# A decoder layer with product-key experts: the norm's share of the expert turns, the projection's opening block, attention's rooms and the queries' end changed

## The reference, cut to what matters

```python
n1 = rms_norm(x, norm1_w) * (1 + sc1) + sh1
h = n1 @ w_in                       # 1024 x 8704: recurrence q|f|i|g, attention q|k|v, two gates
oa = hgrn_chunked(q, 1 - f, i, log f, S0) ; ya = (rms_norm(oa) * silu(g)) @ w_branch_a
ob = three dilated window attentions, merged by their softmax sums ; yb = ob @ w_branch_b
x = x + g1 * ((sigmoid(ga) * ya + sigmoid(gb) * yb) @ w_out)
n2 = rms_norm(x, norm2_w) * (1 + sc2) + sh2
# experts, for every token: 8 heads, each takes the best 16 of 128 x 128 product keys
q = rms_norm((n2 @ peer_wq) per head) ; s1, s2 = q @ k1.T, q @ k2.T ; eidx, g = top16(s1 + s2)
x = x + g2 * sum over heads and picks of g * gelu(n2 . u[eidx]) * v[eidx]
```

## Time and profile before

| what | number |
|---|---|
| median of three runs | 4373.25 us |
| the profiled execution's own time | 4375.05 us |
| its span | 4373.3 us |
| busy in the span | PE 3063.8, DVE 2572.8, ACT 1940.2, POOL 1446.6 us |
| moved by all DMA queues | 1454.06 MB, 332 GB/s over the span |
| moved by the gathers' queue | 1107.36 MB, 62.6% of 16 engines' time |
| mean granted TensorE clock | 0.824 |

### The profile page before, as it was taken

One profiled execution on the slowest core, in us unless ns is written; L12 is line 12 of the kernel. 1 busy time (PEld: TensorE's weight loads), 2 busy tenths in 40 slices (PEclk: granted clock), 3 DMA queues, 4 the chain that ended last, 5 costly groups with the idle time before them and its releaser, 6 DMA issues. The chain is left out here.

```text
span 4373.3 us, 46875 instructions
## 1 busy us (share of the span) xinstructions
PE 3063.8 (70%) x14244; PEld 1663.8 (38%) x14244; DVE 2572.8 (59%) x6558; ACT 1940.2 (44%) x6708; POOL 1446.6 (33%) x1174
## 2 busy tenths in 40 slices
PE   7999877784898998566654686885555556555556
PEld 5677754641553446344432464551111111111111
DVE  2362335377566755584654545467667766766774
ACT  2123431045457844574542225445455555545554
POOL 4453102352332333232211113335244344334432
PEclk9998889886999999666876797887777776777879
DMA  7434245388999999787999988999999999999997
GB/s 281 185 142 138 83 142 179 112 354 335 364 406 377 422 421 401 287 334 274 382 360 361 344 308 312 381 368 386 403 420 420 415 409 420 420 404 419 417 407 308
DMA packets 313887, 1454.06 MB, mean 332 GB/s; under 512 B 41609, under 2 KB 102977, under 8 KB 165282
## 3 DMA queue, kind: packets, MB, share of 16 engines
q0 software_dynamic: 152064, 1107.36, 62.6%
q1 hardware_dynamic: 147118, 336.43, 21.7%
q10 hardware_dynamic: 14452, 7.26, 0.6%
HBM read 1383.55 MB, written 74.57 MB: 333 GB/s over the span
## 5 line engine op out<-in xcount | busy, mean ns | idle before, releaser
L3249 POOL DMA_INDIRECT uv_ring<-in_peer_uv,pick_idx x736 | 794.9, 1080 | 1853.4 <-PE expert_acc L3421 1355.2
L3421 PE MATMUL expert_acc<-uv_ring,diag 128*32 128x512 f32 (+1 forms) x2888 | 714.4, 781 | 424.8 <-ACT diag L3386 373.3
L3344 DVE SCALAR_TENSOR_TENSOR uv_ring<-uv_ring,n_pairs 128x1024 f32<-128x1024 f32 x534 | 651.2, 1232 | 410.0 <-DMA uv_ring<-in_peer_uv,pick_idx 339.1
L3373 ACT ACTIVATE gelu_cube<-dots_now 128x2 f32<-128x2 f32 x528 | 105.7, 200 | 1017.8 <-DVE uv_ring L3344 589.9
L3421 PEld LDWEIGHTS expert_acc<-uv_ring,diag 128*32 128x32 f32 (+1 forms) x2888 | 154.8, 149 | 886.0 <-ACT diag L3386 544.6
L3381 ACT ACTIVATE pick_weight<-gelu_tanh,pick_share 128x1 f32<-128x1 f32 x1056 | 350.9, 379 | 23.1 <-ACT pick_share L3378 4.1
L3421 PE MATMUL expert_acc<-uv_tail,diag 128*64 128x512 f32 x608 | 215.4, 847 | 171.6 <-ACT diag L3386 150.3
L3344 DVE SCALAR_TENSOR_TENSOR uv_ring<-uv_ring,n_more 128x1024 f32<-128x1024 f32 x202 | 243.7, 1222 | 144.8 <-DMA uv_ring<-in_peer_uv,pick_idx 111.6
L997 PE MATMUL h_acc_q<-in_w_all_q,n_all_q 128*128 128x512 f32 x640 | 285.1, 601 | 4.0 <-DVE h_stage_q L971 3.7
L3376 ACT ACTIVATE gelu_tanh<-gelu_cube,dots_now 128x1 f32<-128x1 f32 x1056 | 253.3, 287 | 16.3
L3378 ACT ACTIVATE pick_share<-dots_now,pick_prob 128x1 f32<-128x1 f32 x1056 | 245.4, 280 | 0.0
(11 more groups left out here) (491 smaller groups left out, 5876.7 us busy)
## 6 DMA issues: line engine op xcount, KB each, us to landing
in_w_p<-in_w_in SPq DMA_DIRECT2D x34, 1024.0 KB, 7.4
in_w_all_q<-in_w_in SPq DMA_DIRECT2D x17, 2048.0 KB
ada_w<-in_w_ada SPq DMA_DIRECT2D x10, 2048.0 KB, 8.2
past_keys_q<-in_past_keys SPq DMA_DIRECT2D x16, 1024.0 KB
uv_ring<-in_peer_uv,pick_idx POOLq DMA_INDIRECT x736
shared_room_q<-in_past_values SPq DMA_DIRECT2D x10, 1024.0 KB
score_pair<-scores SPq DMA_DIRECT2D x66, 128.0 KB
wq_raw_p<-in_peer_wq SPq DMA_DIRECT2D x16, 512.0 KB, 5.8
```

Of the source, the lines that this page charges most:

```text
L3249: pool.indirect_dma_start(self.rows_of(part, s), None, self.x["peer_uv"][0], bass.IndirectOffsetOnAxis(ap=self.idx[:, q % 2, 2 * half + s, ...
L3344: ins = dve.scalar_tensor_tensor(out=row, in0=row, scalar=1.0, in1=n2[:, s if tile < LAST_TILE else 0, :], op0=ALU.mult, op1=ALU.mult, acc ...
L3373: link(act.activation(self.cube[:], dots, ACT.Square))
L3421: ins = pe.matmul(self.acc[s * w:(s + 1) * w, c, :], self.diag[:, of % DIAGS, t, 0:w], rows, start=first, stop=last)
```

## The change: what it does

1. **Norm.** In span q's first norm the nominal cost per tile is 5.0 in place of 9.0 on all engines (`share`); other norms keep 9.0.
2. **Opening block.** The projection's block 0 (2 MB) is loaded by SP into the shared room during that norm, behind the first two tiles' rows and the shifts (`SharedRoom.first`). The projection loads blocks 1 and 2 at its start, and block n + 1 from block 2 on. PE takes block 0 out of the room. POOL waits before block 1 until block 0's units are done, and the slot in the room opens at part 41 instead of 33. DVE waits for the rotary tables only before its first QK unit.
3. **Rooms.** The places of raw queries, raw values and the second state output in the shared room are exchanged; the second state output moves into the chunk tables. In attention, SP issues keys(1), the query rows and both past blocks 0 and 1 before it waits for the state stores; the wait now stands before values(1).
4. **Queries' end.** `LAST_TURNS` = 2 further turns are put at the end of the query phase: on PE one after the third of the last head's rows and one behind the head, on the other engines both behind it. `FRONT_PARTS` becomes 259, the tail's slots open two parts later, and `FRONT_US` becomes 2116.87 x 235 / 233, a rate of 0.11007.
5. **Tail picks.** Groups that begin at or behind part 259 do two pick steps a turn in place of one, from the same first turn on.

```diff
@@ -581,6 +581,7 @@
+    share = 9.0 if held is not None else 5.0
@@ -616,7 +617,7 @@
-            beside.sp(9.0)
+            beside.sp(share)
...
@@ -824,7 +825,7 @@
-        terms = (([w_all[:, 0], w_all[:, 1]], n_hi),)
+        terms = ()
@@ -863,19 +864,24 @@
             if not span.split:
-                at_least(sp, unit_done, first[n - 1] if n >= 2 else 0)
+                at_least(sp, unit_done, first[n - 1] if n >= 3 else 0)
                 sp.dma_start(w_all[:, n % 2], w_dram[n]).then_inc(raw_in[n % 2], 16)
...
 
-        load(1 if span.split else 0)
+        load(1)
+        if not span.split:
+            load(2)
         sp.dma_start(weights[:, 0, :], x["q_norm_w"].broadcast_to([P, DH])).then_inc(consts_in, 16)
...
         for n, (_, kind, to) in enumerate(blocks):
-            load(n + (2 if span.split else 1))
+            if span.split:
+                load(n + 2)
+            elif n >= 2:
+                load(n + 1)
             if room is not None and n == len(blocks) - 1:
@@ -909,6 +915,9 @@
         for n in range(len(blocks)):
+            if n == 1 and not span.split:
+                assert beside.other.fetched <= MORE_FROM, beside.other.fetched
+                pool.wait_ge(unit_done, first[1])
             split(n + 2, 0)
@@ -943,12 +952,13 @@
         done = 0
-        dve.wait_ge(consts_in, 16 * (2 + sum(P // w for _, w, _ in tiles)))
         for n, (_, kind, to) in enumerate(blocks):
...
                 if kind == "QK":
+                    if done == 0:
+                        dve.wait_ge(consts_in, 16 * (2 + sum(P // w for _, w, _ in tiles)))
                     done += 1
@@ -978,23 +988,28 @@
                 pe.wait_ge(split_done, 2 * (n + 1))
+                here = [(w_part[b], n_part) for w_part, n_part in terms]
+            elif n == 0:
+                pe.wait_ge(room.w_first_in, 16)
+                here = [(room.w_first, n_hi)]
             else:
-                pe.wait_ge(raw_in[b], 16 * (n // 2 + 1))
+                pe.wait_ge(raw_in[b], 16 * ((n + 1) // 2))
+                here = [(w_all[:, b], n_hi)]
             for u, s, r, (at, t0, k, cost) in numbered(n):
...
                         for h in range(NH):
-                            ins = nc.tensor.matmul(acc[h * k:(h + 1) * k, s, 0:DH], n_hi[:, c, at * P:at * P + k], w_all[:, b, c, h * DH:(h + 1) * DH],
+                            ins = nc.tensor.matmul(acc[h * k:(h + 1) * k, s, 0:DH], n_hi[:, c, at * P:at * P + k], here[0][0][:, c, h * DH:(h + 1) * DH],
                                                    start=(c == 0), stop=(c == DC - 1))
                         continue
-                    for j, (w_part, n_part) in enumerate(terms):
-                        start, stop = c == 0 and j == 0, c == DC - 1 and j == len(terms) - 1
+                    for j, (w_part, n_part) in enumerate(here):
+                        start, stop = c == 0 and j == 0, c == DC - 1 and j == len(here) - 1
                         if kind == "T":
-                            ins = nc.tensor.matmul(acc[:, s, 0:k], w_part[b][:, c, at * P:(at + 1) * P],
+                            ins = nc.tensor.matmul(acc[:, s, 0:k], w_part[:, c, at * P:(at + 1) * P],
                                                    n_part[:, c, t0:t0 + k], start=start, stop=stop)
                         else:
-                            ins = nc.tensor.matmul(acc[0:k, s, 0:WB], n_part[:, c, at * P:at * P + k], w_part[b][:, c, :],
+                            ins = nc.tensor.matmul(acc[0:k, s, 0:WB], n_part[:, c, at * P:at * P + k], w_part[:, c, :],
                                                    start=start, stop=stop)
@@ -1464,16 +1479,21 @@
         unit = lambda k, s: flat[:, (2 * k + s) * BLOCK:(2 * k + s + 1) * BLOCK]
-        self.q_raw, self.v_raw = [unit(0, 1 - s) for s in range(2)], [unit(3, 1 - s) for s in range(2)]
+        self.q_raw, self.v_raw = [unit(0, 1), unit(3, 0)], [unit(3, 1), unit(0, 0)]
         self.k_raw = [[unit(1, 1 - s), unit(2, 1 - s)] for s in range(2)]
-        self.state_out = [self.f_raw[:, 0], self.q_in[:, 0]]
+        self.state_out = [self.f_raw[:, 0], self.tables[:, BLOCK:2 * BLOCK].rearrange("p (h t) -> p h t", h=HEADS)]
         self.reset = self.tables[:, 2 * BLOCK:]
...
         self.masks = self.tables[:, 0:BLOCK].rearrange("p (m t) -> p m t", m=4)
+        self.w_first, self.w_dram = flat[:, 0:DC * span.w_cols].rearrange("p (c w) -> p c w", c=DC), x["w_in"]
+        self.w_first_in = sem("w_first_in")
         self.raw_in, self.row_in = [sem("fq_in0"), sem("fq_in1")], [sem("gv_in0"), sem("gv_in1")]
...
         self.state_stored, self.final_stored = [sem("state_stored0"), sem("state_stored1")], sem("p_state_stored")
+
+    def first(self):
+        self.nc.sync.dma_start(self.w_first, self.w_dram[0]).then_inc(self.w_first_in, 16)
 
@@ -1641,14 +1661,14 @@
             load_values(0, have=1)
-            for s in range(2):
-                sp.wait_ge(room.state_stored[s], 16 * DEC_B // 2)
         load_keys(1)
...
             load_past(0)
+            load_past(1)
+            for s in range(2):
+                sp.wait_ge(room.state_stored[s], 16 * DEC_B // 2)
         load_values(1)
-        load_past(1)
         beside.gap("sp", 3)
@@ -2651,6 +2671,8 @@
                 beside.pe(C_S)
+                if h == PH - 1:
+                    beside.last_row("pe", n)
 
@@ -2736,6 +2758,9 @@
     def after_head(self, name, h):
+        pass
+
+    def last_row(self, name, n):
         pass
@@ -2856,7 +2881,12 @@
     def after_head(self, name, h):
-        pass
+        if h == PH - 1:
+            self.head(name, 1 if name == "pe" else LAST_TURNS)
+
+    def last_row(self, name, n):
+        if name == "pe" and n == 2:
+            self.head(name, LAST_TURNS - 1)
 
@@ -2899,9 +2929,10 @@
 
-FRONT_PARTS = 257
+LAST_TURNS = 2
+FRONT_PARTS = 257 + LAST_TURNS
 PART_SLOTS = 5
-MORE_FROM, MORE_TO = 33, 119
+MORE_FROM, MORE_TO = 41, 119
 QUERY_FROM, QUERY_SLOTS = 226, 2
@@ -2978,7 +3009,7 @@
         return FOUR_STEPS
-    return 2 if PICK_GROUPS[q].steps > PICK_GROUPS[q - 1].parts else 1
+    return 2 if PICK_GROUPS[q].steps > PICK_GROUPS[q - 1].parts or PICK_GROUPS[q].first >= FRONT_PARTS else 1
 
@@ -3462,7 +3493,7 @@
-FRONT_US = 2140.87
+FRONT_US = 2116.87 * (FRONT_PARTS - Opening.TURNS) / (FRONT_PARTS - LAST_TURNS - Opening.TURNS)
@@ -3568,7 +3599,7 @@
-                                phase(norm_phase, tag + "1", busy, span, beside, const, first_gains, n_hi, n_lo, x_rows, None, None)
+                                phase(norm_phase, tag + "1", busy, span, beside, const, first_gains, n_hi, n_lo, x_rows, None, None, room)
```

More of the change, by code:

```diff
@@ L626, in _ @@
         for n, w, at in tiles:
-            beside.pool(9.0)
+            beside.pool(share)
     @block.scalar
@@ L648, in _ @@
                 nc.scalar.copy(n_hi[:, :, n * P:n * P + w], turned[:, n % 2, :, 0:w]).then_inc(copied, 1)
-            beside.act(9.0)
+            beside.act(share)
     @block.vector
@@ L688, in _ @@
                 nc.vector.tensor_tensor(n_lo[part], turned[:, n % 2, :, 0:w], n_hi[part].bitcast(F32), ALU.subtract).then_inc(copied, 1)
-            beside.dve(9.0)
+            beside.dve(share)
     @block.tensor
@@ L698, in _ @@
             ins.then_inc(turned_done, 1)
-            beside.pe(9.0)
+            beside.pe(share)
 def column_blocks(w_cols):
```

## The result

The changed kernel is slower: 4387.6 us in the median of 20 runs against 4374.6 us of the kernel before in as many, a ratio of 1.0026 (95% interval 1.0014 to 1.0037), some 11 us. The forecast was 4368 us and a small gain. The time lies inside the stated range, on the wrong side of no change.

A forecast was written before the change was run, and what follows sets the result against it. Time was taken as bytes at full DMA rate plus DMA idle time. The terms -10.5 + 1 + 0 + 5 - 1 = -5.5 gave 4369.5 us profiled, 4368 against the median; eight-in-ten range 4340 to 4392.

The forecast's parts named there:

- Norm and opening block: Norm and projection's start: less DMA idle, 12 instead of 22.5 us, a gain of 10.5; -9.5 with the slot.
- part 1's account of SP's queue: Norm and opening block: SP's 2 MB load ahead of the third tile's token rows costs 0, or +5 if slower.
- 0; if it takes twice that beside gathers, +5: Norm: load issued near 1040 takes 9 us, is in by 1050, before DVE's third tile rows are due at 1056.
- The two turns are not saved but moved ... Their DVE work there stands beside other work: Norm's two turns go to projection and query phase, where DVE has 413 of 689 and 137 of 267 us.
- +1: Projection: extra slot opens at part 41 instead of 33, ring one slot shallower for eight parts; bounds 0 and +6.
- Projection's end: Last block's loads into the shared room wait for part 119's sum: 0, bounds -4 and +8.
- Attention's order: Attention: SP's earlier loads stand behind the same small packets, its queue not empty while it waits: 0, bounds -11 and +3.
- Queries' end: Two extra turns at the query phase's end: DMA idle about 13 us instead of 8.5, +5, bounds -5 and +16.
- Tail picks: Tail: nearly all of POOL's 393 us of index waits go, mostly covered by ten queued parts: -1, bounds 0 and -21.
- A: Rival: the projection follows PE and its 24.7 us lead stays, -19.7 in all, 4353.5 us; chance 0.23.
- B: Rival at the queries' end: no gather goes out until the rest starts, +19 there, 4382 us; chance 0.20.
- C: Rival in the tail: the pick waits were lost time after all, -21 in place of -1, 4348 us; chance 0.07.

The follow-up runs named there:

- run 9: Changed kernel with the opening block's load behind the last token rows, slot from part 36, SP's turns ahead of the projection's stores: 0.9967 of the kernel before, 4366.2 us.
- run 6: Kernel before with SP's turns ahead of a unit's store in span q's projection: ratio 1.0002 to the kernel before.
- run 3: Changed kernel with the opening block's load issued behind the norm's last token rows: ratio 1.0003 to the kernel before.
- run 2: Changed kernel with the opening block loaded at the projection's start, slot from part 33, no POOL wait at block 1; share stays 5.0: 0.9993 of the kernel before.
- run 5: Changed kernel without the early opening block, and with SP's turns ahead of the stores in span q's projection: ratio 0.9978 to the kernel before.
- run 10: Changed kernel with SP's turns ahead of the stores in span q's projection, nothing else: ratio 0.9991 to the kernel before.
- run 7: Changed kernel with the opening block's load behind the last token rows and the extra slot from part 36 instead of 41: ratio 1.0002 to the kernel before.
- run 4: Kernel before with the extra slot opened at part 41 instead of 33, nothing else: ratio 1.0008 to the kernel before.
- run 1: Changed kernel with norm share 9.0, opening block loaded at the projection's start, slot from part 33; rooms, queries' end, tail picks kept: 0.9993 of the kernel before.
- run 8: Changed kernel without the two extra turns at the queries' end, FRONT_PARTS back at 257: ratio 1.0040 to the kernel before.
- run 11: Changed kernel with one pick step a turn in the tail, as before: ratio 1.0017 to the kernel before.

## Why the prediction was wrong

**Norm and opening block, the step that failed.** Forecast -9.5 us with the slot, measured +11.3. What failed is part 1's account of SP's queue: it put the wait of the third tile's token rows at 0, and it has no term at all for the n2 rows, whose issue moves with the turns. The runs price the first at 9.2 us and the second at 6.2 to 9.2, and the slot at 0 to 4 in place of 1. Beyond what the forecast took for them that is 14 to 22 us together, and 20.8 are missing. The account that these sizes were laid on was sound: in the mended kernel (run 9) n + p is 8.4 us below before, and 6.8 below run 6, which has the same order of SP's turns; the DMA idle of both stages is 28.3 us in place of 36.4.

- "0; if it takes twice that beside gathers, +5" for the token rows behind the 2 MB. It was 9.2 us (after to run 3) by the stages. Two numbers under the 0 were wrong. The load took 14.1 us to land, not 9. And 1056, the time at which DVE would want the rows, was read from the kernel before, where DVE does a turn between the second tile and the third. With the share of 5.0 the first turn comes behind the third tile, so DVE wants the rows already at 1048.5. The timeline of DVE before, that of the changed kernel, and the changed kernel's issue of the load (KB, us from issue to landing):

```profile
1047.77 1.22 DVE L3344 SCALAR_TENSOR_TENSOR uv_ring<-uv_ring,n_pairs 128x1024 f32<-128x1024 f32 x1
...
1056.53 0.15 DVE L672 RECIPROCAL norm_stat_q<-norm_stat_q 128x1 f32<-128x1 f32 x1
...
1047.23 1.23 DVE L679 TENSOR_TENSOR normed_q<-normed_q,shift_p_q 128x1024 f32<-128x1024 f32 x1
...
1061.06 1.22 DVE L3375 SCALAR_TENSOR_TENSOR uv_ring<-uv_ring,n_pairs 128x1024 f32<-128x1024 f32 x1
...
shared_room_q<-in_w_in SPq DMA_DIRECT2D x1, 2048.0 KB, 14.1
```

DVE could begin the third tile at 1058.40, 2 us after the time that the prediction had for it and 10 us after it stood ready. The Trainium skill, "DMA: Bandwidth & Descriptors", "Queues, rings and completion order", has one ring taken in order; the trace of the changed kernel agrees (9.95 us of idle, 2.97 with the load behind the rows). The prediction named this wait and kept 0.

- "The two turns are not saved but moved ... Their DVE work there stands beside other work". The work does, but SP's issues move with the turns, and the prediction followed only DVE's work and the gathers. The n2 rows' load slid behind a store and a weight load on SP's queue: 8.1 us (run 2 to run 5), 9.2 (after to run 10), 6.2 (run 7 to run 9). This alone eats most of the norm's gain.
- "+1" for the slot: 0 to 4 us by run 7, 0 to 5.6 by run 4, inside its bounds of 0 to 6 and near none of them for certain.

**Projection's end.** 0 was right: PE's wait at the last stage buffers was 20.1 us, 17.2 before; the share of that stretch stayed poor in both.

**Attention's order.** 0 by SP's full queue. With the share of 9.0 that holds (run 1: 502.9 us for hgrn and attention, 503.5 before); with 5.0 it can't be told, as the nine kernels with the changed rooms read 496.0 to 507.5.

**Queries' end.** Forecast +5 for the turns; a cost of that size is not there (run 8), and what they are worth beyond that is open. The working of DVE's 15.9 us is right: in the changed kernel its work behind the last score row runs from 2962.9 to 2978.4, 15.5 us. The forecast of the hole was too long: 13 us of DMA idle against 8.5 before. POOL of the changed kernel (timeline):

```profile
2951.96 0.94 POOL L3280 DMA_INDIRECT uv_ring<-in_peer_uv,pick_idx  x1 [0.31 <-issue]
2959.82 0.94 POOL L3280 DMA_INDIRECT uv_query<-in_peer_uv,pick_idx  x1 [6.92 <-PE expert_acc L3452]
...
2963.55 2.46 POOL L3280 DMA_INDIRECT uv_query<-in_peer_uv,pick_idx  x1 [0.31 <-issue]
2980.88 1.49 POOL L3280 DMA_INDIRECT uv_tail<-in_peer_uv,pick_idx  x1 [14.87 <-POOLq L3553]
```

Four gathers go out from 2959.82 on, released by PE's sum between the last score rows. They carry the DMA over the joint, whose windows read:

```profile
2970.00:2980.00 10.00, 3.68 (x8) 0.85 (x8) 8.08 (x23) 2.89 (x12) 0.00 (x0) 0.50 0.84 347
2980.00:2990.00 10.00, 8.99 (x28) 2.79 (x30) 9.28 (x31) 7.70 (x30) 7.12 (x7) 0.70 0.82 313
```

That is 3.7 us of idle; before, the share was 0.24 from 2950 to 2960, some 8 us of idle. But the turns alone don't explain it. The same joint without the turns in run 8, and below it with the turns in run 1 (windows):

```profile
2961.00:2971.00 10.00, 0.97 (x8) 0.37 (x12) 0.47 (x1) 0.87 (x4) 0.35 (x1) 0.50 0.63 253
2971.00:2981.00 10.00, 6.36 (x24) 1.17 (x16) 7.06 (x19) 4.06 (x17) 7.56 (x9) 0.50 0.86 302
...
2965.00:2975.00 10.00, 3.34 (x8) 0.85 (x8) 8.44 (x24) 2.89 (x12) 0.00 (x0) 0.67 0.26 109
2975.00:2985.00 10.00, 7.78 (x26) 2.42 (x28) 8.93 (x29) 7.69 (x30) 6.90 (x7) 0.76 0.77 295
```

Run 8 idles 5.4 us there without the turns, and run 1, which has them with the norm's share of 9.0, idles 10. So how full the DMA is at this joint depends also on what the changed norm and opening move, and not on these two turns alone.

**Tail picks.** -1 forecast, 0 to -1.5 measured, with all 393 us of waits gone: a wait of POOL is not a wait of the DMA. In the changed kernel too the share falls to 0.13 at the end (window 4355 to 4360), as in the earlier trace rows; before, this remnant lasts some 15 us, from 4344 to 4358, and not the tens of us that the prediction made of it. The Trainium skill ("DMA: Bandwidth & Descriptors", "Latency and other measured facts") has DMA engines 7 and 15 usually slower than the others. A share of 0.13 fits two of sixteen, but the rows don't say which, and no run here tests the cause.

**Rivals.** A did not come: PE's lead was 15.8 us at its first matmul and nothing at the first QK units (1270 us in both kernels). B did not: 17.3 us lie between the last front gather (2963.55) and the first tail gather (2980.88), where over 25 was its sign. C did not (run 11). The slower side came from a mechanism that was not among them.

## What to carry to other kernels

When work is handed out by a running count, a change of that count in one phase moves every later turn against its phase, on every queue: list the DMAs that the moved turns issue and what then stands ahead of them. A due time read from the old timeline is no longer good where a moved turn stood ahead of it. A load that fills an idle stretch belongs behind whatever small transfers the stretch itself is waiting for on the same queue. A wait costs mostly what reaches beyond the transfers already in flight: here one of 18 us left the DMA idle for 3.6 us, one of 23 us for 10.

## What was not expected of the hardware

The eight loads of n2 rows (1 MB) took 17 to 23 us from their last issue to their landing beside a full queue of gathers at a DMA share near 1.0. What stood ahead of them on SP's queue goes with the difference: 17.1 us with 2 MB of weights issued behind them (1343.92 to 1361.01 before), 19.1 with the weights issued 17 us ahead (1364.85 to 1383.97 in the changed kernel), 23.3 with the weights issued 5 us ahead (1337.57 to 1360.87 in run 5). So run 5 issues the rows 9 us before DVE stands and DVE still waits 13.95 us.
